# Linear attention of two mixing stages without chunk states, all convolution taps on VectorE, and a reordered last step

## The chip, the cores and the metric

One core of a Trainium2 chip runs the whole program. The metric is the device time of one execution in microseconds (us); lower is better. TensorE (PE) multiplies matrices, VectorE (DVE), ScalarE (ACT) and GpSimd (POOL) do elementwise work, SyncE (SP) issues the transfers of the weights. Semaphores order the engines among each other; each engine runs its own instructions strictly in program order.

## The reference

256 tokens of width 1024 go through two blocks of two layers each. The first block (a gated MLP, an attention with relative bias, two SwiGLU layers) is untouched. Each of the second block's two layers is a mixing stage and a gated feed-forward stage. A mixing stage projects the tokens with `w_in`, and then computes three things side by side: a causal depthwise convolution with 31 taps over 256 channels, then a layer norm; a causal softmax attention with 4 heads ("moba"); and a gated linear attention with 4 heads (key width 64, value width 128). Their outputs are joined and multiplied by `w_out`. The linear attention is, in the reference, in chunks of 32 tokens:

```
G = jnp.cumsum(gc, axis=3)                  # within a chunk
qg = qc * jnp.exp(G); kg = kc * jnp.exp(-G); kd = kc * jnp.exp(gamma - G)
attn = jnp.where(tril, einsum("bhnid,bhnjd->bhnij", qg, kg), 0.0)
d_state = einsum("bhnjd,bhnje->bhnde", kd, vc)
state <- decay[..., None] * state + d_state          # scan over 8 chunks
o = einsum("bhnij,bhnje->bhnie", attn, vc) + einsum("bhnid,bhnde->bhnie", qg, s_prev)
```

## The kernel before, in words

**Weights and tiles.** All weights come as a stream of 206 units of 128x2048 floats, each 1 MB, through four slots. For every unit U, ACT rounds it to fp32r (`hi(U)`, line 489), DVE forms the remainder (`lo(U)`, line 947), and PE uses both, with three products for each tile (`split3`, lines 1499 to 1501: hi times hi, hi times lo, lo times hi). SP issues the transfer of unit U+4 once `lo(U)` is done (line 341). PE can use a unit only after its `lo`, so the place of each `lo` in DVE's order is a due time for PE. Tokens lie in two halves of 128 (`m` = 0, 1).

**The mixing stage** (lines 1760 to 2020 on PE, one loop pass per layer `l`). U0 is its first unit. PE runs `step(0)` to `step(5)`, each a product of the tokens with 512 columns (step 4: 256), over 8 tiles `kt` for m0 and again for m1. Step 2 uses units U0+4 and U0+5, step 3 U0+6 and U0+7, step 4 U0+8, step 5 U0+9 and U0+10; each unit but U0+8 holds half of the `kt` (0 to 3 or 4 to 7). The dictionaries `m0`, `m1` of a step name small pieces of PE work that run behind a given `kt`. After step 5 comes `out_product` with units U0+11 to U0+14, turns (j, q), with hooks of its own.

**The small pieces on PE** are: `conv_turn` and `logits`; `cumsum` (line 1827, the running sum of the log gates by a product with the block-triangular `tri`); `qk_turn` (transposes of q and k); `kd_turn` (transposes of the decayed keys, kept by ACT as `kdt`); `gla_scores` (line 1844); `state_inc(n)` (line 1859, the increment of the state by chunk n, n = 0 to 6, each four products, each after the state two chunks back has been updated); `gla_out(b)` (lines 1885 and 1891: for each token half and head pair one product of the masked scores with the values, then one product for each of the chunks with its state, 28 in the two calls); `mqk_turn`, `moba_scores`, `moba_turn`, `moba_pv` for the softmax attention; `ln_turn`, `ln_back` around the layer norm of the convolution; `y_turn`, `mo_turn` for the outputs.

**DVE** runs, in one hand-written order (lines 1217 to 1420), the `lo` of units U0+2 to U0+16, the taps, the exponent products, the masking of the scores (`copy_predicated`, line 1286, eight of 128 columns), `state(n)` (lines 1299 and 1301), the softmax preparation `moba_begin`, and the head norms. A tap (lines 1242 and 1246) multiplies a shifted window of `hpad` by one weight and adds it to `cacc`: both inputs lie in SBUF. Of the 31 taps of the first 128 channels (a = 0) all are on DVE; of those of the second (a = 1), the first 20 are on **POOL** (`POOL_TAPS`, lines 444 to 452: a multiply into `ptap`, then an add into `cacc2`) and 11 on DVE, which then adds `cacc2` (line 1319). So DVE has 42 taps per layer, 22 of them alternating between the two halves, and 20 of the first half in a row.

**ACT** runs the `hi` of the units, copies PSUM results to SBUF (`keep`, line 766), and evaluates the exponentials and other functions.

Of the kernel before, what the change touches and what calls it, by code (L numbers as in the profile page):

```python
# [19 lines left out]
P = 128  # L20
# [8 lines left out]
SEQ = 256  # L29
# [14 lines left out]
NCH = SEQ // GCH  # L44
RANK = 16
# [17 lines left out]
POOL_TAPS = 20  # L63
# [14 lines left out]
def two_blocks_kernel(nc, x_in, stream, cols, bs_col, ws_t, gs_row, fin_row, fin2_row, rel_rows, ffn_cw,  # L78
                      conv_w, conv_ln, moba_g, gla_g, gate_w, gate_b, gate_in, out):
    ctx = ExitStack()  # L80
    with ctx:
# [33 lines left out]
        def const(name, shape, dt=F32):  # L115
# [7 lines left out]
        tri = const("tri", [P])  # L123
        ones = const("ones", [P])
# [11 lines left out]
        dec = const("dec", [2, NCH])  # L136
# [45 lines left out]
        kdt = at("kdt", [M, 256], o_sc + 5184)  # L182
# [3 lines left out]
        st_g = at("st_g", [NCH - 1, 2, P], o_sa)  # L186
# [14 lines left out]
        ptap = at("ptap", [SEQ], o_sc + 8768)  # L201
        cacc2 = at("cacc2", [SEQ], o_sb + 3200)
# [48 lines left out]
        x_qktr, x_G, x_e1, x_gd, x_e2, x_qg, x_kd, x_kdtr, x_kdc = (  # L251
            sem("gla_" + n) for n in ("qk_transposed", "G_kept", "exp_G", "G_diff", "exp_diff", "q_decayed", "k_decayed",
                                      "kd_transposed", "kd_kept"))
        x_at0, x_A, x_Am, x_dS, x_St, x_o, x_oc = (
            sem("gla_" + n) for n in ("masked_zeroed", "scores", "scores_masked", "state_inc", "state", "o", "o_kept"))
# [5 lines left out]
        x_pm, x_pa, x_tap1 = sem("conv_pool_product"), sem("conv_pool_sum"), sem("conv_tap_second")  # L261
# [90 lines left out]
        def _(pool):  # L352
# [13 lines left out]
            t3 = tri[:, :].rearrange("p (b c) -> p b c", c=GCH)  # L366
            pool.affine_select(out=t3, in_=t3, compare_op=ALU.is_ge, fill=0.0, base=0,
# [25 lines left out]
            pool.dma_start(glg[:, :, :], gla_g).then_inc(consts_loaded, 16)  # L393

# [33 lines left out]
            for l in range(2):  # L428
# [13 lines left out]

                pool.wait_ge(x_cpad, l + 1)
                for i in range(POOL_TAPS):
                    dst = ptap if i else cacc2
                    if i > 1:
                        pool.wait_ge(x_pa, (POOL_TAPS - 1) * l + i - 1)
                    pool.tensor_scalar(dst[:, :], hpad[:, 1, i:i + SEQ], cw[:, l, 1, i:i + 1], None,  # L448
                                       ALU.mult).then_inc(x_pm, 1)
                    pool.wait_ge(x_pm, POOL_TAPS * l + i + 1)  # L450
                    if i:
                        pool.tensor_tensor(cacc2[:, :], cacc2[:, :], ptap[:, :], ALU.add).then_inc(x_pa, 1)
# [22 lines left out]
        def _(act):  # L475
# [250 lines left out]
            for l in range(2):  # L726
# [25 lines left out]
                hi(U0 + 4)  # L752

# [7 lines left out]
                hi(U0 + 5)  # L761
# [13 lines left out]
                flat = [z[:, :, :].rearrange("p a t -> p (a t)") for z in (gG, eG, nG, dG)]  # L775
                act.activation(flat[0], tb[3][:, :], ACT.Copy).then_inc(x_G, 1)
                act.activation(flat[1], tb[3][:, :], ACT.Exp, scale=1.0 / TAU).then_inc(x_e1, 1)
                act.activation(flat[2], tb[3][:, :], ACT.Exp, scale=-1.0 / TAU).then_inc(x_e1, 1)
                hi(U0 + 7)
                act.wait_ge(x_gd, l + 1)  # L780
                act.activation(flat[3], flat[3], ACT.Exp, scale=1.0 / TAU).then_inc(x_e2, 1)
# [37 lines left out]
                moba_exp(0)  # L819
# [7 lines left out]

                o_keep(0)
                moba_exp(1)
                o_keep(1)  # L830
# [109 lines left out]
        def _(dve):  # L940
# [269 lines left out]
            for l in range(2):  # L1210
# [19 lines left out]
                first = [(0, i) for i in range(TAPS)]  # L1230
                second = [(1, i) for i in range(POOL_TAPS, TAPS)]
                order = []
                while first:
                    order += [first.pop(0)] + ([second.pop(0)] if second else [])

                def taps(n0, n1):
                    for a, i in order[n0:n1]:
                        src = hpad[:, a, i:i + SEQ]
                        w = cw[:, l, a, i:i + 1]
                        i0, done, n = (0, x_tap, TAPS) if a == 0 else (POOL_TAPS, x_tap1, TAPS - POOL_TAPS + 1)  # L1240
                        if i == i0:
                            dve.tensor_scalar(cacc[:, a, :], src, w, cw[:, l, a, TAPS:TAPS + 1], ALU.mult,
                                              ALU.add).then_inc(done, 1)
                        else:
                            dve.wait_ge(done, n * l + i - i0)
# [12 lines left out]
                lo(U0 + 5)  # L1258
                taps(9, 14)
# [8 lines left out]
                e4 = eG[:, :, :].rearrange("p a (n c) -> p a n c", c=GCH)  # L1268
                dve.tensor_copy(dec[:, :, :], e4[:, :, :, GCH - 1]).then_inc(x_qg, 1)
                dve.wait_ge(x_qktr, 2 * l + 2)  # L1270
                dve.wait_ge(x_qg, 3 * l + 1)
                ef, nf, df = (z[:, :, :].rearrange("p a t -> p (a t)") for z in (eG, nG, dG))
                dve.scalar_tensor_tensor(ef, tb[1][:, :], float(DK) ** -0.5, ef, ALU.mult, ALU.mult).then_inc(x_qg, 1)
                dve.tensor_tensor(nf, tb[2][:, :], nf, ALU.mult).then_inc(x_qg, 1)
                taps(14, 17)
# [867 lines left out]
```

## Time and profile before

| | |
|---|---|
| Time, median of 3 runs | 1272.89 us (1270.46 to 1273.14) |
| Time of the profiled execution | 1270.38 us, of which the span of the trace 1268.7 us |
| Busy PE / DVE / ACT / POOL | 1245.9 (98%) / 816.0 (64%) / 664.3 (52%) / 141.7 us (11%) |
| Granted clock of TensorE | full (2.4 GHz) throughout |
| Transfers | 220.13 MB, 174 GB/s on average |

The two mixing stages end their products at about 760 and 1066 us of the span; the stretches in question are 660 to 750 us (layer 0) and 967 to 1057 us (layer 1). In the rows, a start time is in us from the start of the span, then comes the duration; `x8` says that eight neighbouring records were merged. An fp32 product is two MATMUL records; a transpose and an fp32r product are one. The duration of a record holds its latency; what one costs in a row of many is the distance between starts.

### The profile page before, as it was taken

The page shows a single profiled execution, that of the slowest core. Times are in us where ns is not written, and L with a number is a line of the kernel's source. Part 1 is how long each engine was busy: PE and PEld are TensorE (multiplying, and loading weights), DVE is VectorE, ACT ScalarE, POOL GpSimd, SP SyncE. Part 2 cuts the span into 40 slices and gives each one's busy share as a digit, 9 for nine tenths or more (in the row PEclk, how much of TensorE's full clock was granted, in tenths as well). Part 3 has the DMA queues.
Part 4 walks back from the last instruction along what each step waited for, and adds up shares of the span by engine and source line. Part 5 has one row for each costly group of instructions (what it writes and reads, how often), then busy time and mean ns, then how long its engine had stood idle before and what let it go on. Part 6 is the DMA issues. An engine that isn't in the chain of part 4 may idle for free.

```text
span 1268.7 us, 16607 instructions
## 1 busy us (share of the span) xinstructions
PE 1245.9 (98%) x6276; PEld 1027.1 (81%) x6276; DVE 816.0 (64%) x926; ACT 664.3 (52%) x800; POOL 141.7 (11%) x164
## 2 busy tenths in 40 slices
PE   7999999999999989999999999999999999999998
PEld 5888888888898768888887788888888777888886
DVE  5466455545567565555469976777746987687763
ACT  6545264434366554444347356676536554666652
POOL 2000000000010000000029610000003930000000
PEclk9999999999999999999999999999999999999999
DMA  9544454446364236445634235544562424554440
GB/s 346 211 182 179 170 197 178 169 186 232 133 249 154 96 122 240 170 170 216 225 112 161 100 129 203 199 161 170 185 223 103 166 95 166 199 183 157 189 183 33
DMA packets 32534, 220.13 MB, mean 174 GB/s; under 512 B 4000, under 2 KB 4032, under 8 KB 6752
## 3 DMA queue, kind: packets, MB, share of 16 engines
q1 hardware_dynamic: 29952, 212.35, 45.2%
q0 software_dynamic: 1664, 5.41, 1.4%
q10 hardware_dynamic: 864, 1.61, 0.4%
q8 instruction: 39, 0.64, 0.2%
q14 instruction: 15, 0.12, 0.0%
HBM read 218.31 MB, written 1.05 MB: 173 GB/s over the span
## 4 chain that ended last, share of the span: by engine, by line
PE 95%; DVE 3%; ACT 1%; DMA 0%; issue 0%; POOLq 0%; POOL 0%; ACTq 0%
PE acc L1499 28%; PE acc L1501 27%; PE acc L1500 27%; PE tb L1531 5%; DVE wlo L947 1%; PE acc L1686 1%; PE acc L1688 1%; PE acc L1689 1%; DVE cacc L1246 1%; PE tb L1859 1%; PE tb L1600 1%; PE tb L1721 1%; PE acc L1885 0%; PE tb L1740 0%; PE acc L1891 0%; DMA x<-in_x_in 0%
## 5 line engine op out<-in xcount | busy, mean ns | idle before, releaser
L947 DVE TENSOR_TENSOR wlo<-raw,whi 128x2048 fp32r<-128x2048 f32 x200 | 458.1, 2310 | 237.4 <-ACT whi L489 237.4
L489 ACT ACTIVATE whi<-raw 128x2048 fp32r<-128x2048 f32 x200 | 376.8, 1907 | 109.2 <-PE acc L1501 100.9
L1499 PE MATMUL acc<-whi,xth 128*128 128x512 f32 (+1 forms) x1056 | 419.1, 397 | 4.4 <-DVE xtl L969 2.2
L1501 PE MATMUL acc<-whi,xtl 128*128 128x512 f32 (+1 forms) x1056 | 409.2, 387 | 0.0
L1500 PE MATMUL acc<-wlo,xth 128*128 128x512 f32 (+1 forms) x1056 | 408.4, 387 | 0.0
L1499 PEld LDWEIGHTS acc<-whi,xth 128*128 128x128 f32 x1056 | 198.7, 188 | 50.0 <-issue 5.8
L1501 PEld LDWEIGHTS acc<-whi,xtl 128*128 128x128 f32 x1056 | 198.6, 188 | 41.3
L1500 PEld LDWEIGHTS acc<-wlo,xth 128*128 128x128 f32 x1056 | 199.0, 188 | 36.8
L1499 PE MATMUL acc<-whi,yth 128*128 128x512 f32 x512 | 202.2, 395 | 1.7 <-DVE ytl L1380 1.7
L1501 PE MATMUL acc<-whi,ytl 128*128 128x512 f32 x512 | 199.7, 390 | 0.0
L1500 PE MATMUL acc<-wlo,yth 128*128 128x512 f32 x512 | 199.5, 390 | 0.0
L1499 PEld LDWEIGHTS acc<-whi,yth 128*128 128x128 f32 x512 | 96.2, 188 | 22.8 <-issue 3.7
L1501 PEld LDWEIGHTS acc<-whi,ytl 128*128 128x128 f32 x512 | 96.1, 188 | 20.4
L1500 PEld LDWEIGHTS acc<-wlo,yth 128*128 128x128 f32 x512 | 96.2, 188 | 19.0
L1428 DVE SCALAR_TENSOR_TENSOR cv<-tb,fcw,cv 128x255 f32<-128x255 f32 (+1 forms) x176 | 72.7, 475 | 14.5 <-ACT cv L875 11.9
L1070 DVE SCALAR_TENSOR_TENSOR yy<-acc,stat,sg 128x256 f32<-128x256 f32 x44 | 20.9, 479 | 80.6 <-ACT sg L596 80.6
L596 ACT ACTIVATE sg<-acc,stat 128x256 f32<-128x256 f32 x44 | 20.5, 472 | 88.8 <-PE acc L1501 88.7
L448 POOL TENSOR_SCALAR ptap<-hpad,cw 128x256 f32<-128x256 f32 x38 | 62.2, 1636 | 3.7
L494 ACT ACTIVATE xth<-xg 128x512 fp32r<-128x512 f32 x32 | 20.0, 633 | 78.2 <-DVE xg L957 78.2
L866 ACT ACTIVATE us<-acc,stat 128x512 f32<-128x512 f32 x44 | 30.5, 693 | 57.5 <-PE acc L1501 57.5
L373 POOL TENSOR_SCALAR stat<-stat 128x2 f32<-128x2 f32 x9 | 2.7, 295 | 418.3 <-ACT junk L503 418.3
L1246 DVE SCALAR_TENSOR_TENSOR cacc<-hpad,cw,cacc 128x256 f32<-128x256 f32 x80 | 48.7, 639 | 1.0
(238 smaller groups left out, 1030.2 us busy)
## 6 DMA issues: line engine op xcount, KB each, us to landing
raw<-in_stream SPq DMA_DIRECT2D x200, 1024.0 KB, 4.8
rb<-in_rel_rows POOLq DMA_DIRECT2D x8, 256.0 KB, 2.9
raw<-in_stream SPq DMA_DIRECT2D x4, 256.0 KB, 4.9
raw<-in_stream SPq DMA_DIRECT2D x2, 512.0 KB, 8.1
gs_sb<-in_gs_row POOLq DMA_DIRECT2D x1, 1024.0 KB, 5.4
frow<-in_fin_row POOLq DMA_DIRECT2D x2, 512.0 KB, 5.4
x<-in_x_in ACTq DMA_DIRECT2D x2, 256.0 KB, 5.0
x<-in_x_in ACTq DMA_DIRECT2D x1, 512.0 KB, 7.3
```

Source lines behind the costliest of these rows:

```text
L448: pool.tensor_scalar(dst[:, :], hpad[:, 1, i:i + SEQ], cw[:, l, 1, i:i + 1], None, ALU.mult).then_inc(x_pm, 1)
L489: act.activation(whi[:, s, :], raw[:, s, :], ACT.Copy).then_inc(hi_ready, 1)
L596: act.activation(sg[:, j % 2, m, :], pair_bank(j + pair, m)[:, 0:256], ACT.Silu, scale=rms(STATS[k], m)).then_inc(g_silu, 1)
L866: act.activation(us[:, j % 2, m, :], pair_bank(j + pair, m)[:, :], ACT.Copy, scale=rms(r1, m)).then_inc(f_ev, 1)
L947: dve.tensor_tensor(wlo[:, s, :], raw[:, s, :], whi[:, s, :], ALU.subtract).then_inc(lo_ready, 1)
L1070: dve.scalar_tensor_tensor(yy[:, j % 2, m, :], pair_bank(j + pair, m)[:, 256:512], rms(STATS[k], m), sg[:, j % 2, m, :], ALU.mult, ALU.mul ...
L1246: dve.scalar_tensor_tensor(cacc[:, a, :], src, w, cacc[:, a, :], ALU.mult, ALU.add).then_inc(done, 1)
L1428: o = dve.scalar_tensor_tensor(dst, src, fcw[:, l, bass.ds(16 * j + 4 * a + tap + 32 * t, 1)], dst, ALU.mult, ALU.add)
L1499: pe.matmul(o, xh, wh, start=first, stop=False)
L1500: pe.matmul(o, xh, wl, start=False, stop=False)
L1501: return pe.matmul(o, xl, wh, start=False, stop=last)
L1531: return pe.transpose(o, i, ident[0:n, 0:n])
```

## The change

It does three things.

1. **Linear attention without states.** `kd_turn`, `kdt`, `state_inc`, `state` and the products with the states are gone. The scores within a token half are completed instead: besides the old products of `nG` with `eG` (same chunk), there are products of the keys decayed to the end of their chunk (`dG`) with the queries of the next chunk (distance one, 16 small ones of 32x32), of `kB` with `qB` (the first two chunks with the last two, 8 of 64x64), and, for the first token half with the second, of `kC` with `qC` (4 of 128x128, kept by ACT as `aX`). `kB`, `qB`, `kC`, `qC` are `dG` and `eG` times a table of factors `ftab`, the exponential of 12 extra columns that `cumsum` gets from the widened constant `trb`; four DVE products make them. `gla_out` is then four products of the scores for each b, plus two of `aX`. The scores are masked by the whole triangle, with one `copy_predicated` for each b. `cumsum` now writes banks 0 and 1, the transposed q and k and the scores banks 2 and 3.
2. **All 62 taps on DVE**, alternating between the two channel halves; POOL has none. `cacc2`, `ptap` and the add of line 1319 are gone.
3. **Order.** `hi(U0+5)` on ACT comes before the logarithm of the gates, `lo(U0+4)` and `lo(U0+5)` on DVE before the first tap, all scores behind `kt` 3 of m1 of step 3. In step 5, both `gla_out` run earlier, `ln_turn` and the second `moba_scores` at the end of m0, the transposes and products of the softmax attention are moved to other `kt`, and `y_turn(0)` goes into the output product. ACT squares the head outputs (`o_square`), and does both `moba_exp` after them.

```diff
-POOL_TAPS = 20
@@ gpsimd
-                for i in range(POOL_TAPS):
...
-                    pool.tensor_scalar(dst[:, :], hpad[:, 1, i:i + SEQ], cw[:, l, 1, i:i + 1], None,
-                                       ALU.mult).then_inc(x_pm, 1)
...
-                        pool.tensor_tensor(cacc2[:, :], cacc2[:, :], ptap[:, :], ALU.add).then_inc(x_pa, 1)
@@ scalar
                 hi(U0 + 4)
+                hi(U0 + 5)
                 act.wait_ge(x_z, l + 1)
...
+                act.activation(ftab[:, :, :].rearrange("p (a m) c -> p (a m) c", m=M), Gt, ACT.Exp,
+                               scale=1.0 / TAU).then_inc(x_tab, 1)
...
                 hi(U0 + 8)
-                act.wait_ge(x_kdtr, l + 1)
-                act.activation(kdt[:, :, :].rearrange("p m c -> p (m c)"), tb[0][:, :], ACT.Copy).then_inc(x_kdc, 1)
                 hi(U0 + 9)
+                act.wait_ge(x_X, l + 1)
+                act.activation(aX[:, :, :, :].rearrange("p b a t -> p b (a t)"), tb01[:, :, 0:2 * P], ACT.Copy).then_inc(x_Xc, 1)
...
                 o_keep(0)
+                o_square(0)
+                o_keep(1)
+                o_square(1)
+                moba_exp(0)
                 moba_exp(1)
@@ vector
+                order = [(a, i) for i in range(TAPS) for a in range(2)]
...
+                lo(U0 + 4)
+                lo(U0 + 5)
                 dve.wait_ge(x_cpad, l + 1)
-                taps(0, 5)
-                lo(U0 + 4)
-                taps(5, 9)
+                taps(0, 9)
...
-                lo(U0 + 5)
-                taps(9, 14)
+                taps(9, 20)
                 lo(U0 + 6)
...
-                taps(14, 17)
+                taps(20, 26)
                 lo(U0 + 7)
...
+                dve.tensor_tensor(kb4, k5[:, :, 0:2, :], factor(0, 0, 2, 1), ALU.mult).then_inc(x_kb, 1)
+                dve.tensor_tensor(qb4, q5[:, :, 2:4, :], factor(2, 0, 2, 1), ALU.mult).then_inc(x_kb, 1)
+                dve.tensor_tensor(kc4, k5[:, 0:4:2, :, :], factor(4, 0, 4, 2), ALU.mult).then_inc(x_kb, 1)
+                dve.tensor_tensor(qc4, q5[:, 1:4:2, :, :], factor(8, 1, 4, 2), ALU.mult).then_inc(x_kb, 1)
+                taps(26, 36)
                 lo(U0 + 8)
...
+                taps(36, 42)
                 lo(U0 + 9)
-                state(0)
...
+                taps(42, 48)
                 lo(U0 + 10)
+                taps(48, 62)
@@ tensor
+                def gla_scores():
+                    pe.wait_ge(x_kb, 4 * l + 4)
...
+                    for m, a, b in both:
+                        c, t = (2 * m + a) * P, m * P
+                        for e in (0, 2 * GCH):
+                            k0, q0 = t + e, t + e + GCH
+                            pe.matmul(tb[2 + b][e:e + GCH, c + e + GCH:c + e + 2 * GCH], dG[rows[b], a, k0:k0 + GCH],
+                                      eG[rows[b], a, q0:q0 + GCH], start=True, stop=True)
...
-                step(3, m0={5: kd_turn}, end=all_of((gla_scores, (0,)), (gla_scores, (1,))),
-                     m1={5: lambda: state_inc(0)})
-                state_inc(1)
+                step(3, m1={3: gla_scores})
...
+                step(5, m0={1: lambda: gla_out(0), 3: lambda: moba_scores(0), 5: lambda: gla_out(1),
+                            7: all_of((ln_turn, ()), (moba_scores, (1,)))},
+                     m1={2: lambda: moba_turn(0), 4: ln_back, 5: all_of((moba_pv, (0,)), (moba_turn, (1,))),
+                         7: lambda: moba_pv(1)})
...
-                            pe.wait_ge(x_oc, 2 * l + 2)
+                            pe.wait_ge(x_osq, 2 * l + 2)
...
-                    (0, 2): lambda: y_turn(1), (1, 2): mo_turn})
+                    (0, 0): lambda: y_turn(0), (0, 2): lambda: y_turn(1), (1, 2): mo_turn})
```

## Rows read from the trace of the kernel before

**Rows 1.** The page: its first line, and the ended-last chain by engine.
```profile
span 1268.7 us, 16607 instructions
...
PE 95%; DVE 3%; ACT 1%; DMA 0%; issue 0%; POOLq 0%; POOL 0%; ACTq 0%
```

**Rows 2.** The waits of PE, whole span: total us, times, longest.
```profile
PE acc L1499 <- DVE wlo L947: 1.9, 2, 1.6
PE acc L1499 <- DVE ytl L1380: 1.7, 2, 0.9
```

**Rows 3.** Timeline of PE (start, duration, line) around the waits for `lo(U0+5)`.
```profile
678.10 0.39 PE L1501 MATMUL acc<-whi,xtl 128*128 128x512 f32 x1
680.13 0.50 PE L1499 MATMUL acc<-whi,xth 128*128 128x512 f32 x1 [1.65 <-DVE wlo L947]
...
987.00 0.50 PE L1499 MATMUL acc<-whi,xth 128*128 128x512 f32 x1 [0.29 <-DVE wlo L947]
```

**Rows 4.** The chain that ended last, 640 to 760 us: start, us, what.
```profile
694.51 0.44 PE tb L1531 x4
696.35 1.64 PE tb L1844 x16
...
702.30 0.58 PE tb L1859 x8
...
722.67 0.42 PE acc L1885 x2
723.09 0.35 PE acc L1891 x8
...
724.22 0.86 PE tb L1931 x8
```

**Rows 5.** Timeline of PE: around `state_inc(0)`, around `gla_out(0)`, first use of U0+7.
```profile
692.99 0.39 PE L1499 MATMUL acc<-whi,xth 128*128 128x512 f32 x1
...
701.91 0.39 PE L1501 MATMUL acc<-whi,xtl 128*128 128x512 f32 x1
...
702.81 0.50 PE L1499 MATMUL acc<-whi,xth 128*128 128x512 f32 x1
...
703.61 0.40 PE L1499 MATMUL acc<-whi,xth 128*128 128x512 f32 x1
...
721.11 0.45 PE L1885 MATMUL acc<-gv,aT 128*128 128x128 f32 x2
...
724.14 0.93 PE L1931 MATMUL tb<-mkT,mqT 64*128 64x128 f32 x8
```

**Rows 6.** Busy time of the instructions on `cacc`, in layer 0's stretch of taps.
```profile
669.55:720.90 51.35, 0.25 (x3) 0.28 (x4) 25.32 (x43) 15.87 (x19) 1.00 0.40 144
```

**Rows 7.** Timeline of DVE: `lo(U0+7)`; two taps and the add, POOL then idle.
```profile
689.27 2.82 DVE L947 TENSOR_TENSOR wlo<-raw,whi 128x2048 fp32r<-128x2048 f32 x1
...
719.16 0.48 DVE L1246 SCALAR_TENSOR_TENSOR cacc<-hpad,cw,cacc 128x256 f32<-128x256 f32 x1
719.68 0.48 DVE L1246 SCALAR_TENSOR_TENSOR cacc<-hpad,cw,cacc 128x256 f32<-128x256 f32 x1
720.09 0.42 DVE L1319 TENSOR_TENSOR cacc<-cacc,cacc 128x256 f32<-128x256 f32 x1
```

**Rows 8.** Timeline of DVE: eight taps of the feed-forward convolution, an input in PSUM.
```profile
785.25 3.34 DVE L1428 SCALAR_TENSOR_TENSOR cv<-tb,fcw,cv 128x255 f32<-128x255 f32 x8 [1.26 <-ACT cv L875]
```

**Rows 9.** Line 947, ns min/median/max: 400 to 640 us, then 676 to 700 us.
```profile
L947 DVE TENSOR_TENSOR wlo<-raw,whi x40: 2280/2291/2294, 398.3 to 638.5; 128x2048 fp32r<-128x2048 f32 x40
...
L947 DVE TENSOR_TENSOR wlo<-raw,whi x4: 2816/2824/2827, 677.3 to 696.9; 128x2048 fp32r<-128x2048 f32 x4
```

**Rows 10.** Timeline of POOL: multiplies of two taps.
```profile
678.03 2.84 POOL L448 TENSOR_SCALAR ptap<-hpad,cw 128x256 f32<-128x256 f32 x1
...
681.79 0.97 POOL L448 TENSOR_SCALAR ptap<-hpad,cw 128x256 f32<-128x256 f32 x1
```

**Rows 11.** Timeline of ACT behind the first softmax copies: table load; second softmax copies.
```profile
731.06 1.28 ACT L835 ACT_TABLE_LOAD   x1
...
735.33 0.60 ACT L813 ACTIVATE pt<-tb 128x512 f32<-128x512 f32 x1 [0.72 <-PE tb L1531]
```

More of the change, by code:

```diff
@@ L250, in two_blocks_kernel @@
                                       "log", "log_a", "cumsum"))
[L251 to L255, printed above, removed]
+        x_qktr, x_G, x_tab, x_e1, x_gd, x_e2, x_qg, x_kd, x_kb = (
+            sem("gla_" + n) for n in ("qk_transposed", "G_kept", "factors", "exp_G", "G_diff", "exp_diff", "q_decayed",
+                                      "k_decayed", "far_scaled"))
+        x_at0, x_A, x_Am, x_X, x_Xc, x_o, x_oc = (
+            sem("gla_" + n) for n in ("masked_zeroed", "scores", "scores_masked", "cross", "cross_kept", "o", "o_kept"))
         x_osq, x_oss, x_oms, x_or, x_ytr, x_yg, x_yh, x_yl = (
@@ L1228, in _ @@
                 o.then_inc(x_z, 1)
[L1230 to L1234, printed above, removed]
+                order = [(a, i) for i in range(TAPS) for a in range(2)]
                 def taps(n0, n1):
@@ L1239, in taps @@
                         w = cw[:, l, a, i:i + 1]
[L1240 to L1241 removed]
+                        done = x_tap1 if a else x_tap
+                        if i == 0:
                             dve.tensor_scalar(cacc[:, a, :], src, w, cw[:, l, a, TAPS:TAPS + 1], ALU.mult,
@@ L1848, in state_inc @@
-                def state_inc(n):
-                    m, p = n // 4, slice(GCH * (n % 4), GCH * (n % 4) + GCH)
-                    if n == 0:
-                        pe.wait_ge(x_kdc, l + 1)
-                        pe.wait_ge(x_ev, 10 * l + 4)
-                    if n >= 2:
-                        pe.wait_ge(x_St, (NCH - 1) * l + n - 1)
+                def gla_scores():
+                    pe.wait_ge(x_kb, 4 * l + 4)
+                    both = [(m, a, b) for m in range(M) for a in range(2) for b in range(2)]
+                    rows = [slice(DK * b, DK * b + DK) for b in range(2)]
+                    for m, a, b in both:
+                        c, ts = (2 * m + a) * P, slice(m * P, (m + 1) * P)
+                        pe.matmul(tb[2 + b][:, c:c + P], nG[rows[b], a, ts], eG[rows[b], a, ts], start=True, stop=True)
+                    for m, a, b in both:
+                        c, t = (2 * m + a) * P, m * P
[3 more added lines that the diff above has]
+                                      eG[rows[b], a, q0:q0 + GCH], start=True, stop=True)
+                    for m, a, b in both:
+                        c = (2 * m + a) * P
+                        mm = pe.matmul(tb[2 + b][0:2 * GCH, c + 2 * GCH:c + P], kB[rows[b], 2 * a + m, :],
+                                       qB[rows[b], 2 * a + m, :], start=True, stop=True)
+                        if m and a:
+                            mm.then_inc(x_A, 1)
@@ L1986, in _ @@
                                     wlo[:, s, ws], kt == 0, kt == KT - 1)
-                        if m == 0 and kt == 3:
-                            state_inc(2)
                     mm.then_inc(m0_done if m == 0 else unit_used, 1)
@@ L1991, in _ @@
                         mqk_turn()
-                        state_inc(3)
-                state_inc(4)
-                step(5, m0={1: lambda: state_inc(5), 3: all_of((state_inc, (6,)), (moba_scores, (0,))),
-                            5: all_of((ln_turn, ()), (gla_out, (0,)), (moba_scores, (1,))),
-                            7: all_of((gla_out, (1,)), (moba_turn, (0,)))},
-                     m1={1: ln_back, 3: all_of((moba_pv, (0,)), (moba_turn, (1,))), 6: lambda: moba_pv(1), 7: lambda: y_turn(0)})
+                step(5, m0={1: lambda: gla_out(0), 3: lambda: moba_scores(0), 5: lambda: gla_out(1),
+                            7: all_of((ln_turn, ()), (moba_scores, (1,)))},
+                     m1={2: lambda: moba_turn(0), 4: ln_back, 5: all_of((moba_pv, (0,)), (moba_turn, (1,))),
+                         7: lambda: moba_pv(1)})
                 def mix_ready(j):
```

159 lines of the change are left out of this document (64 added, 95 removed).

## The prediction

> **What bounds the kernel now.** I read the page first: the chain that ended last is 95% PE and 3% DVE [rows 1], so what counts is PE's work and the few places where PE waits. The waits of PE are next. In the whole span only two kinds touch the mixing stages: two for the remainder of a weight unit, together 1.9 us, and two for the last remainder of the linear attention's output, together 1.7 us [rows 2]. The first kind is `lo(U0+5)`: PE is through with unit U0+4 at 678.10 + 0.23 = 678.33 and goes on at 680.13, that is 1.80 lost with the restart; in layer 1 the row shows 0.29, with the restart 0.45 [rows 3]. In layer 1 PE comes 1.35 us later to the same place, because DVE's order there starts at the same event and PE has done more before it. Then I read DVE between 669.55 and 720.90: it has no gap there that matters, and the instructions on `cacc` alone, 43 of them, take 25.3 of its 51.35 us, 0.59 each [rows 6]. So DVE is the second limit: it is not waited for often, but it delivers the units only just in time. `lo(U0+7)` ends at 689.27 + 2.82 = 692.09 and PE wants it at 692.99 [rows 5, 7]. Whoever puts more on DVE there must say what comes off.
>
> **PE work, per layer.** Prices are distances on the path. An insertion among the large products also costs a lead and a slow restart: around `state_inc(0)` PE goes from 701.91 + 0.23 to 702.81, and the next three products take 0.80 instead of 0.68, so 0.67 + 0.12 = 0.79 for an insertion of which 0.58 is the work [rows 4, 5]. The overhead is then 0.2.
> Removed: `state_inc` seven times. Five stand alone at about 0.79, two share an insertion and cost about 0.68: 5.3 us. `gla_out` takes 721.11 to 724.14, 3.03, and the second call the same: 6.0 [rows 5]. `kd_turn` 0.44 [rows 4]. The old scores 1.64 + 0.2 = 1.85 [rows 4]. Sum 13.6.
> Added, scores: the old eight, 1.64 (0.205 each with 128 stationary columns [rows 4]); the four of `kC` at the same price, 0.82; the eight of 64x64 at the price of a state increment, 0.58 / 4 = 0.145: 1.16; the sixteen of 32x32. No row has that shape. The nearest is a product with a state, 32 stationary columns and 128 moving: four take 0.35, 0.09 each [rows 4]. Its upper bound is a full product, 0.205, its lower bound one half of the nearest row, 0.045. I take 0.10: 1.6. A change of shape also costs something: a full product between the small ones takes 0.42 instead of 0.205 [rows 4]; three such changes, 0.6, and the insertion 0.2. Sum 6.0, with bounds of 4.5 (small ones at 0.045, no cost for changes) and 8.2 (all at 0.205 with changes).
> Added, output: twelve full products at 0.205 = 2.46, and one more insertion than before, 0.2: 2.7.
> Net: 8.7 − 13.6 = −4.9 us per layer, between −6.4 and −2.7. The 12 extra columns of `cumsum` I cost at nothing: 16 records of 128 columns take 1.64, 0.10 each, well above what so few columns need while the stationary load sets the pace; if not, it is under 0.1.
> The Trainium skill (TensorE: Matmul & The Clock Gate, LDWEIGHTS) says that loading the stationary operand costs by its columns and not by its rows. The rows' falling prices for 128, 64 and 32 columns agree; an estimate from its formula would put the small products near 0.06 each and the sum lower by about 0.7 a layer.
>
> **The taps, and what POOL did to DVE.** Twenty more taps at 0.59 would be 12 us more on DVE, and that would sink the change. But the trace says that 0.59 is not the price of a tap. With POOL idle (from 718.9 on) a tap lasts 0.48; two in a row on the same sum start 0.52 apart (the second waits for the first), and the next instruction starts 0.41 behind [rows 7]. Eight taps of the feed-forward convolution, which alternate over four outputs, take 3.34, so 0.40 each [rows 8]. The new order alternates between two sums, so every tap finds its predecessor done. I take 0.40, with 0.52 as the upper bound; 62 taps are then 24.7 us, against 25.3 for 42 taps and the add. The cause is a lock between DVE and POOL: where they meet, a POOL multiply of 0.97 takes 2.84 while a `lo` runs [rows 10], and four `lo` in a row take 2.82 instead of 2.29 [rows 9]; those 4 x 0.53 = 2.1 us come back too.
> The Trainium skill (SBUF — State Buffer, Who interferes with whom) says that a DVE instruction with two SBUF inputs and a GpSimd instruction that reads SBUF exclude one another for their whole length. By that rule, the trace agrees, for taps and `lo` alike.
> DVE also loses the states (about 3.9 with the copy of the decay), 0.34 for the add and 1.2 for the square, which ACT takes; it gains four products of 256 columns, 1.4 at the 0.34 that the add occupies. So DVE has about 7 us less to do in each layer, though 20 taps more.
>
> **Due times, walked through in layer 0** (start 669.55, as before). On DVE: `lo(U0+4)` to 671.8 and `lo(U0+5)` to 674.0; 9 taps to 677.4, log gates 678.0, 11 taps 682.3, `lo(U0+6)` 684.6, three products 686.3, 6 taps 688.7, `lo(U0+7)` 691.0; the last decay product and the four new ones to 693.1, 10 taps 697.0, `lo(U0+8)` 699.2. On PE: unit U0+5 is there at 678.33, so the wait of 1.80 (0.45 in layer 1) is gone. `cumsum` at 679.7 finds its input of 678.1, 1.6 before. Step 3 starts at 688.4 (`lo(U0+6)` 684.6). **It wants `lo(U0+7)` at 691.1 and gets it at 691.0: no margin in layer 0, 1.4 in layer 1.** The scores at 696.5 find their four inputs of 693.1. The scores last to 702.5. Their mask waits for them on DVE from 699.2 to about 702: behind that wait are 26 taps and `lo(U0+9)`, `lo(U0+10)`; mask to 703.2, then 705.6, 707.8 (U0+9), 710.2, 712.4 (U0+10), last tap 718.0. PE wants U0+9 at 712.3 and U0+10 at about 717, and `ln_turn` comes at 721.4. All in time. ACT waits for the cross scores before it copies `aX`; behind it are both keeps of `mqk` and `hi(U0+10)`. That is 702.6 to 703.2 and not in the way: the second `mqk` is finished by PE only at 705.3.
> **What is late next.** The tail of step 5 is packed more tightly. After `ln_turn` come the statistics, the second softmax preparation, its exponentials and copy, then on ACT a table load, the silu and three more, 4.3 us, before the second softmax copy (731.06 to 735.33 [rows 11]). That chain is 10.1 us long after `ln_turn`, and PE has 9.6 of work: a wait of 0.5 before `moba_pv(1)`. From there to `y_turn(1)` DVE and ACT need 6.6 (hi, lo, gain, sums, gating), PE 6.15: another 0.5. Both are estimates by the same walk. The old wait of 0.9 for the last remainder [rows 2] stays: its loop behind `y_turn(1)` is unchanged.
> POOL's new memsets run once, among the loads of the constants, before anyone needs them: nothing.
>
> **Sum.** −2 x 4.9 = −9.8; −1.80 − 0.45 = −2.25; new waits 2 x 1.0 = +2.0. Together −10.0. The profiled execution took 1270.4, so 1260.4; against the median of the runs, 1272.9, it would be 1262.9. The profiled time lies at the lower edge of the runs, so I put the forecast between: **1261.5**, own range 1257.5 to 1265.5.
>
> **Rivals.**
> *DVE becomes the bound* (slower). If the slow taps were not POOL's doing, 62 taps at 0.60 would put `lo(U0+7)` at 696.1, 5.0 us after PE wants it, and the last tap at 727.8, 6.4 after `ln_turn` is due; `moba_begin(0)` is queued behind the taps, one more us. The output product would go on at about 748.9 where it does at 746.9 now: +2 per layer, 1274.5 on the profiled scale, 1275.5 forecast. It decides from about 0.57 per tap. For it: 0.59 is what 42 taps show [rows 6]. Against: 0.48 and 0.40 where POOL is idle or the second input is not SBUF [rows 7, 8]. Chance 0.07.
> *Half way*: taps at 0.52, as for two on one sum. 24 such taps before `lo(U0+7)` are 2.9 late, 1.5 in layer 1, and as the last tap then ends just as `ln_turn` is due, about 5 us of the gain go: 1266.5. A variant of it is the Trainium skill's rule (VectorE: DVE Perf Modes, The DRAIN you can't avoid) that the next instruction does not start before the pipe is empty. In this kernel that would be 0.48 per tap, the duration in [rows 7], 1.9 us more before `lo(U0+7)`, and 1264.5; the 0.40 of [rows 8] speaks against it. Chance 0.07 for the first, 0.04 for the variant.
> *The small products are dear*: scores at 8.2 instead of 6.0, +2.2 per layer, 1266. Chance 0.08.
> *Several unseen waits in the repacked step 5*, 4 us and more per layer, so that nothing measurable is left: 1270 to 1272. For it: every due time there is my walk, and ACT's order in that stretch is new. Chance 0.04.
> *The forecast*: 0.70.
>
> **How the numbers follow.** From the low bound of the small products (−1.5 a layer, 1258) with a little more, 1257, to the half-way and dear cases with some of their spread, 1268: outside are the slow rival and no change, and a little below. A difference under 0.2% (2.5 us) can't be told from none. Slower by more than that 0.07; within it 0.04; the rest, faster, 0.89.
>
> **What would show it.** Taps of about 0.40 and `lo` of 2.29 throughout the stretch; no wait for `lo(U0+5)`; a wait of at most some tenths for `lo(U0+7)`; the scores in one block of about 6.0 us and `gla_out` of about 1.3 each; waits of about 0.5 at `moba_pv(1)` and `y_turn(1)`. Layer 0 shorter by about 5.7, layer 1 by about 4.3. It is wrong if taps stay near 0.6, if PE waits for `lo(U0+7)` by microseconds, or if the scores take 8.

## The result and the profile after

| | before | after |
|---|---|---|
| Median | 1271.73 us (1270.46 to 1273.14, 4 runs) | 1256.78 us (1254.33 to 1257.39, 4 runs) |
| Ratio, 95% interval | | 0.9877 (0.9865 to 0.9889) |
| Profiled execution, span | 1268.7 us | 1252.6 us |

The change takes 15.0 us off where 11.4 were forecast. The time, 1256.78, lies 0.2 us below the widest range of the prediction (1257 to 1268) and 0.7 below the one that stands with its sum (1257.5 to 1265.5). Of the 11.4, the worked sum gave 10.0; the rest came from putting the forecast between the profiled execution and the median. The page after, its first two lines and the chain by engine:

```profile
span 1252.6 us, 16325 instructions
...
PE 1230.3 (98%) x6172; PEld 1020.8 (81%) x6172; DVE 803.5 (64%) x928; ACT 665.6 (53%) x806; POOL 45.7 (4%) x92
...
PE 94%; DVE 3%; ACT 2%; issue 0%; DMA 0%; POOLq 0%; POOL 0%; DVEq 0%; ACTq 0%
```

PE still sets the time (compare [rows 1]). It has 15.6 us less to do, and DVE, with 40 taps more in the two layers, has 12.5 less (about 14 were forecast). Where the time goes is seen in the stretch that the change touches. I take it from the first product of the gate to the start of `mo_turn`, in both layers: first before, then after. Each line gives the start and end, the length, the busy time of PE with its records, and the granted clock (1.00 is the full 2.4 GHz).

```profile
660.13:751.07 90.94, 88.42 (x555) 1.00 0.36 128
968.35:1057.94 89.59, 88.44 (x555) 1.00 0.36 130
```

```profile
660.38:742.51 82.13, 80.71 (x503) 1.00 0.40 141
959.84:1041.88 82.04, 80.62 (x504) 1.00 0.39 142
```

The stretches are 8.81 and 7.55 shorter, together 16.4, against 16.1 in the span: nothing else of note changed. These two lengths are the finer measure below, because the executions of one kernel differ by 2 to 3 us. The traces show a reason outside the stretches: in seven of the experiments TensorE's granted clock falls to 1.2 GHz for 3.4 us or more at 447 to 449 us, behind a wait of 2.9 us, and in the other runs, with the same wait, it doesn't. Two experiments have such a fall inside a stretch as well; it is named there.

The waits of PE after, those in the stretch:

```profile
PE acc L1491 <- DVE ytl L1372: 1.8, 2, 0.9
...
PE tb L1523 <- DVE og L1359: 1.1, 2, 0.5
```

Each line gives the total in us, the times and the longest. The wait for a unit [rows 2] is gone, the old one of 0.9 per layer for the last remainder stands, and 0.5 per layer before `y_turn(1)` is new. The scores on PE (layer 0), from the start of the block to the next large product:

```profile
696.96 1.16 PE L1831 MATMUL tb<-eG,nG 64*128 64x128 f32 x16
698.06 0.46 PE L1836 MATMUL tb<-eG,dG 64*32 64x32 f32 x32
698.44 0.68 PE L1840 MATMUL tb<-qB,kB 64*64 64x64 f32 x16
699.05 0.71 PE L1846 MATMUL tb<-qC,kC 64*128 64x128 f32 x8
699.70 0.50 PE L1491 MATMUL acc<-whi,xth 128*128 128x512 f32 x1
```

By the distances between starts: 1.10 for the eight full products (1.64 before [rows 4]), 0.38 for the sixteen small ones, 0.61 for the eight of 64x64, 0.65 for the last four; 2.74 in all. With 0.09 between the last large product and the block, and 0.12 for the large products' slow restart behind it, it is 2.95. The forecast had 6.0. Here is the error.

On DVE, all taps and the `lo` between them:

```profile
L1258 DVE SCALAR_TENSOR_TENSOR cacc<-hpad,cw,cacc x120: 464/477/502, 674.9 to 1014.1; 128x256 f32<-128x256 f32 x120
...
L963 DVE TENSOR_TENSOR wlo<-raw,whi x3: 2281/2282/2284, 682.6 to 697.3; 128x2048 fp32r<-128x2048 f32 x3
...
709.88 5.65 DVE L1258 SCALAR_TENSOR_TENSOR cacc<-hpad,cw,cacc 128x256 f32<-128x256 f32 x14
715.43 0.43 DVE L1321 SCALAR_TENSOR_TENSOR pp<-tb,cmask 128x256 f32<-128x256 f32 x1
```

Fourteen taps in 715.43 − 709.88 = 5.55, 0.396 each; `lo` at 2.28; before, with POOL at work, they took 0.59 and 2.82 [rows 6, 9].

### The profile page after: what moved, and what is told of

It reads as the page before. It is cut to its first block, busy times and chain, and to the rows that moved or that the text cites. A ratio compares the mean times of both kernels' runs of the same rounds, so it can differ in the third digit from the quotient of the medians.

```text
span 1252.6 us, 16325 instructions
## 1 busy us (share of the span) xinstructions
PE 1230.3 (98%) x6172; PEld 1020.8 (81%) x6172; DVE 803.5 (64%) x928; ACT 665.6 (53%) x806; POOL 45.7 (4%) x92
## 4 chain that ended last, share of the span: by engine, by line
PE 94%; DVE 3%; ACT 2%; issue 0%; DMA 0%; POOLq 0%; POOL 0%; DVEq 0%; ACTq 0%
PE acc L1491 27%; PE acc L1493 27%; PE acc L1492 27%; PE tb L1523 5%; PE acc L1678 1%; PE acc L1680 1%; PE acc L1681 1%; DVE wlo L963 1%; ACT whi L493 1%; PE tb L1592 1%; PE tb L1713 1%; PE tb L1732 0%; DMA x<-in_x_in 0%; ACT pp L814 0%; PE acc L1871 0%
## 5 line engine op out<-in xcount | busy, mean ns | idle before, releaser
L891 ACT ACTIVATE cv<-tb,fcw 128x256 f32<-128x256 f32 x88 | 42.6, 565 | 10.5 <-PE tb L1523 10.5
L969 DVE TENSOR_TENSOR x<-acc,x 128x512 f32<-128x512 f32 x32 | 21.7, 685 | 25.5 <-PE acc L1493 25.5
```

Source lines behind the costliest of these rows:

```text
L891: o = act.activation(cv[:, j % 2, a, :], tb[2 * (j % 2) + a // 2][:, (a % 2) * SEQ:(a % 2 + 1) * SEQ], ACT.Identity, scale=fcw[:, l, bass. ...
L969: dve.tensor_tensor(xs, out_bank(OUT_PAIR[k], m, c)[:, :], xs, ALU.add).then_inc(n_add, 1)
```

## The experiments

The theory after the result: the walk on DVE was right, and the scores were over-priced, because (A) products that alternate between two row groups (the halves of 64 rows, `b` = 0 and 1) overlap the load of one with the work of the other, and (B) small products are cheap. Rival causes: sizes alone; less lost to DVE than thought; the new order worth more than I gave it. Unless said otherwise, an experiment changes the kernel after, and the lengths of its two stretches stand against 82.13 and 82.04: "+0.94 and +0.93" means layer 0 and layer 1, in us. Medians stand against 1256.78.

**The order of the row groups.**

```diff
-                    both = [(m, a, b) for m in range(M) for a in range(2) for b in range(2)]
+                    both = [(m, a, b) for b in range(2) for m in range(M) for a in range(2)]
```

> The changed kernel with one edit: the scores are computed for all of the first row group (partitions 0 to 63) and then for all of the second (64 to 127), in each of their first three parts, instead of alternating. Same products, same shapes. Theory A (the alternation of row groups lets the load of one product's stationary operand overlap the other's work): the eight full products go from 1.10 back to 1.64 us as in the kernel before, the 64x64 ones from 0.61 to about 1.1, the small ones from 0.38 to about 0.6 or more; the block of scores from 2.74 to about 4.0, +1.3 us per layer, +2.5 in all (1259.3). Theory B (the scores are cheap because of their sizes, not their order): the block stays at 2.7 and the time at 1256.8.

```profile
699.81 1.71 PE L1831 MATMUL tb<-eG,nG 64*128 64x128 f32 x16
701.45 0.60 PE L1836 MATMUL tb<-eG,dG 64*32 64x32 f32 x32
701.98 0.96 PE L1840 MATMUL tb<-qB,kB 64*64 64x64 f32 x16
702.87 0.72 PE L1846 MATMUL tb<-qC,kC 64*128 64x128 f32 x8
703.52 0.50 PE L1491 MATMUL acc<-whi,xth 128*128 128x512 f32 x1
```

The eight full products are back at 1.64, to the hundredth, the small ones take 0.53, the middle ones 0.89; the block is 3.71, +0.97. The stretches are +0.94 and +0.93. The median, 1257.28 us, does not resolve it. Order counts, with 0.97 of the 3.05 us that were missing per layer; the rest are prices of small and middle products that are below the forecast's in either order, and the 0.6 for changes of shape.

How the order acts can be read from the starts of the single records. The two lines show the records that are under way at one moment of the eight full products, first in the kernel after, then here:

```profile
697.18 0.39 PE L1831 MATMUL tb<-eG,nG 64*128 64x128 f32 x4
700.14 0.38 PE L1831 MATMUL tb<-eG,nG 64*128 64x128 f32 x2
```

In the kernel after, the starts come in pairs, 0.007 apart, with 0.112 from pair to pair. Here they come singly, 0.112 apart, and a second series, also at 0.112, starts at 700.36 while the first still has three records to start. So a row group keeps the same pace in both orders; what the alternation does is to let both groups work side by side from the first product on, and here they do so only where the series happen to meet. Theory A is right that the groups overlap, but it is more than a load behind a product: the products themselves run together. The old price of 0.205 was thus an average of stretches with one group and with two.

**The same in the kernel before**: its eight score products alternate.

```diff
-                step(3, m0={5: kd_turn}, end=all_of((gla_scores, (0,)), (gla_scores, (1,))),
+                step(3, m0={5: kd_turn}, end=gla_scores,
```

(with `gla_scores` looping over `m`, `a`, `b`, the latter innermost; one execution)

> The kernel before with one edit: its eight score products alternate between the two row groups. Theory A: they take 1.1 instead of 1.64 us, -0.5 per layer. Theory B: they stay at 1.64, as the shapes are unchanged. One us in all is too little for the whole time; the block in the profile decides.

```profile
698.98 1.16 PE L1844 MATMUL tb<-eG,nG 64*128 64x128 f32 x16
700.08 0.50 PE L1499 MATMUL acc<-whi,xth 128*128 128x512 f32 x1
```

1.10 where it was 1.64 [rows 4]: 0.137 per product instead of 0.205, for shapes and data that are the same. The starts show the same two patterns, pairs every 0.112 here and single records 0.112 apart before.

The Trainium skill says (TensorE: Matmul & The Clock Gate, The mechanism) that a stationary load overlaps running products only if it goes to another row group. Both runs agree that a change of row group makes such products faster, and the prediction had passed that sentence over. The "only" isn't borne out: the large products of 256 columns use all rows, start 0.12 apart after the block of scores, and have a load record of 0.19 each between them.

The 0.54 did not reach the time. The stretches are 90.98 and 89.67, so +0.04 and +0.08 against the kernel before, where the expectation had 0.5 less per layer. PE comes earlier to the state increments and waits for DVE there, 0.3 us in each layer, which is new:

```profile
PE tb L1860 <- DVE st_g L1299: 0.7, 2, 0.3
```

**The price of the small products**: the sixteen issued five times over (one execution).

```diff
-                    for m, a, b in both:
+                    for m, a, b in 5 * both:
```

> The changed kernel, with the sixteen 32x32 products issued five times over (the same result is written again). It measures their price: 64 more per layer. By the changed kernel's profile (0.38 us for 16, 0.024 each) the set of 80 takes 1.9 us, +1.5 per layer, +3.1 in all. By the price that the prediction took from the nearest row (0.10 each) it would be 8 us for 80, +6.4 per layer, +13 in all; by its lower bound (0.045) 3.6.

```profile
700.09 1.56 PE L1836 MATMUL tb<-eG,dG 64*32 64x32 f32 x160
701.57 0.68 PE L1840 MATMUL tb<-qB,kB 64*64 64x64 f32 x16
```

Eighty take 1.48, so 64 more cost 1.10, 0.017 each, and layer 0's stretch is +1.10. The prediction had 0.10 each and a lower bound of 0.045. The single records agree: four start within 0.02, and the next four 0.032 later, and a product is two records, so one costs 0.016. In layer 1 the stretch is +3.50: a gap that no semaphore explains lies among the small products there.

```profile
1000.45 1.52 PE L1836 MATMUL tb<-eG,dG 64*32 64x32 f32 x156
1004.23 0.25 PE L1836 MATMUL tb<-eG,dG 64*32 64x32 f32 x4 [2.26 <-issue]
...
q8 instruction: 1, 0.02, 4.1%
```

It is in no other kernel's list of PE's waits, and the granted clock is full there. The last line is from the transfers between 1001 and 1003 us: one of 16 KB on the queue for instructions, started at 1001.58, lasting 1.30 us. In layer 0 such a transfer started at 701.72, behind the small products. That would fit a long run of short products that gets ahead of the supply of its instructions, but no run varies it, so the cause stays open.

**Changes of shape**: full and small products mixed (one execution).

```diff
+                            for b in range(2):
+                                pe.matmul(tb[2 + b][:, c:c + P], nG[rows[b], a, ts], eG[rows[b], a, ts], start=True,
...
+                            for e in (0, 2 * GCH):
+                                k0, q0 = t + e, t + e + GCH
+                                for b in range(2):
```

> The changed kernel with the full and the 32x32 score products mixed (two full, four small, four times over), row groups still alternating. The prediction charged 0.2 us for each change of shape, seen around the full products of the old output, which use all 128 rows. If shape changes cost that, seven more changes add about 1.4 us per layer to the block of scores (2.74 to 4.1, +2.8 in all). If it was not the shape but the rows (a product over all 128 rows shares rows with its neighbours, so its load can't overlap them), nothing changes: 2.7, the full and small ones together about 1.5.

```profile
699.99 0.49 PE L1833 MATMUL tb<-eG,nG 64*128 64x128 f32 x4
700.41 0.26 PE L1838 MATMUL tb<-eG,dG 64*32 64x32 f32 x8
...
702.46 0.68 PE L1843 MATMUL tb<-qB,kB 64*64 64x64 f32 x16
```

Full and small together take 2.47 instead of 1.48, and the stretches are +0.95 each. With six more changes of shape (seven in place of one) that is 0.16 for each: between my two theories, nearer to the first. So shapes do matter, if less than the 0.2 charged, and the change keeps their number to three.

**GpSimd's taps back**: the second part undone, 20 taps on POOL and 42 on DVE.

```diff
-                taps(0, 9)
+                taps(0, 6)
...
+                dve.tensor_tensor(cacc[:, 1, :], cacc[:, 1, :], cacc2[:, :], ALU.add).then_inc(x_tap1, 1)
```

(and POOL's loop of the kernel before)

> The changed kernel with its second part undone: 20 taps of the second channel half on GpSimd again, 42 on VectorE in the old order and the add behind them, spread over the same places in proportion. If the lock between the two engines was what made a tap 0.6 us: taps at 0.60 and the remainders of units that GpSimd meets at 2.8; lo(U0+7) ends about 693 and PE waits for it by 1 to 2 us in layer 0; GpSimd ends its taps at about 719, when ln_turn is due at 718.5, another 1 us: +2 to +5 us (1259 to 1262). If the taps' price does not depend on GpSimd: VectorE has 20 taps less at 0.40, is early everywhere, and only GpSimd's end counts: +0 to +2.

```profile
680.26 4.80 DVE L1276 SCALAR_TENSOR_TENSOR cacc<-hpad,cw,cacc 128x256 f32<-128x256 f32 x8
684.98 2.83 DVE L977 TENSOR_TENSOR wlo<-raw,whi 128x2048 fp32r<-128x2048 f32 x1
...
694.38 0.50 PE L1513 MATMUL acc<-whi,xth 128*128 128x512 f32 x1 [1.28 <-DVE wlo L977]
```

1261.33 us, 4.6 above the kernel after; stretches +3.10 and +1.85. Eight taps take 4.72, 0.59 each, alternating as they do in the kernel after, where they take 0.40. Alternating alone does not make them fast; POOL has to be silent as well. With 20 taps fewer DVE is later, and PE waits for it. The wait shown is for `lo(U0+7)`. There is none for `lo(U0+5)`, although the taps are slow: the third part of the change, which puts that `lo` ahead of the taps, removes it by itself.

**The second part alone**, in the kernel before.

```diff
-POOL_TAPS = 20
...
+                order = [(a, i) for i in range(TAPS) for a in range(2)]
...
-                taps(17, 24)
+                taps(22, 34)
```

> The kernel before with the second part of the change alone: all 62 taps on VectorE, alternating, none on GpSimd; the states, scores and order as before, taps spread over the old places. Theory A (a tap costs 0.40 without GpSimd): VectorE is no later anywhere than before although it has 20 taps more, lo(U0+5) ends about 678.2, so the wait for it shrinks from 1.8 us to about 0 in layer 0 and from 0.45 to 0 in layer 1, and PE's work is unchanged: -2 us (1269 to 1270.5). Theory B (a tap costs 0.6 wherever it is): +12 us of work on VectorE per layer, PE waits by several us: 1280 and more.

1270.27 us beside 1272.52, ratio 0.9983 (0.9973 to 0.9992). The stretches are 1.76 and 0.75 shorter than before, and neither wait of PE for a unit is listed. So moving 20 taps onto the busier of two engines made the kernel faster by about what I had booked for the waits (1.80 and 0.45).

**Taps in a row**: first one channel half, then the other.

```diff
-                order = [(a, i) for i in range(TAPS) for a in range(2)]
+                order = [(a, i) for a in range(2) for i in range(TAPS)]
```

> The changed kernel with the taps in another order: 31 of one channel half, then 31 of the other, so each waits for the one before it. The prediction priced that at 0.52 per tap against 0.40. If so, lo(U0+7) comes about 3 us later, PE waits for it 2.7 us in layer 0 and 1 to 2 in layer 1, and the last tap ends 7 us later, about 722.5, 4 us after ln_turn is due, of which 3 are taken up by the earlier wait: +3 to +4 per layer, +6 to +8 in all (1263 to 1265). If the distance stays 0.40, no change.

```profile
674.63 4.13 DVE L1258 SCALAR_TENSOR_TENSOR cacc<-hpad,cw,cacc 128x256 f32<-128x256 f32 x8
678.68 0.68 DVE L1268 SCALAR_TENSOR_TENSOR la<-la,tmp 128x512 f32<-128x512 f32 x1
...
PE acc L1491 <- DVE wlo L963: 4.2, 2, 2.8
...
695.00:698.40 3.40, 3.40 (x9) 0.50 0.90 308
```

1265.64 us, +8.9; stretches +5.51 and +3.79. A tap costs 4.05 / 8 = 0.51, as read from [rows 7], and PE waits 2.8 and 1.4 us for `lo(U0+7)`, then for the last tap and for ACT's softmax copies. The price was right, its consequence somewhat worse than expected (9.3 in the two stretches for 6 to 8); the prediction's half-way rival gave this case 5. The last line shows a side effect: behind the wait of 2.8 the granted clock fell to 0.50 (1.2 GHz) for 3.4 us, and eight large products took 3.39 where eight take 1.82 at full clock. Little of it counts: the last tap ended at 722.66 and `ln_turn` began at 723.01, so at full clock PE would have waited for the tap instead. Behind the wait of 1.4 in layer 1 the clock did not fall.

**The order of the first units undone.**

```diff
-                lo(U0 + 4)
-                lo(U0 + 5)
                 dve.wait_ge(x_cpad, l + 1)
-                taps(0, 9)
+                taps(0, 5)
+                lo(U0 + 4)
+                taps(5, 9)
```

> The changed kernel with the order of the first units undone: lo(U0+4) behind 5 taps, lo(U0+5) behind the log gates, hi(U0+5) behind the logarithm. With fast taps lo(U0+5) ends at about 678.2, when PE wants it at 678.6 (layer 0 of the changed kernel), so almost nothing: within 0.5 us (1256.3 to 1257.3). If the new place of lo(U0+5) was what removed the wait of 1.8 + 0.45 us, +2 us (1259).

1256.64 us; stretches +0.40 and −0.03, and no wait for `lo(U0+5)` is listed. Its earlier place is worth nothing that the median shows and at most 0.4 us in layer 0: the fast taps remove that wait too. With slow taps (above) the place alone does. Either suffices, and the two gains don't add.

**Step 5's order undone.**

```diff
-                step(5, m0={1: lambda: gla_out(0), 3: lambda: moba_scores(0), 5: lambda: gla_out(1),
-                            7: all_of((ln_turn, ()), (moba_scores, (1,)))},
+                step(5, m0={3: lambda: moba_scores(0), 5: all_of((ln_turn, ()), (gla_out, (0,)), (moba_scores, (1,))),
+                            7: all_of((gla_out, (1,)), (moba_turn, (0,)))},
```

> The changed kernel with step 5's order undone: the small pieces of PE, and the copies and exponentials on ACT, at the places of the kernel before; y_turn(0) before the output product. If the new order is worth something, it is by the waits behind ln_turn, which comes two tiles earlier in the old order but finds everything else later: I expect within 1 us of the changed kernel, either way (1255.8 to 1257.8). Rival: the old order makes ACT's second output copy wait as before, 1 us per layer more (1259).

```profile
PE tb L1523 <- DVE cacc L1258: 2.0, 2, 1.2
```

1255.99 us; stretches +0.37 and 0.00. `ln_turn` now waits for the last tap (2.0 in all), and the wait before `y_turn(1)` is gone in exchange. Of the third part, these two places are worth at most 0.4 us each, and only in layer 0. The place of all the scores behind `kt` 3 of m1 was not undone, so nothing is shown about it.

**Two tries at the waits that are left.** In both, the square of the softmax outputs comes ahead of `hi(U0+12)`. First, `lo(U0+12)` later:

```diff
                 gated(0)
-                lo(U0 + 12)
-                y_gain(0)
...
+                y_gain(0)
                 gated(1)
+                lo(U0 + 12)
                 y_lo(0)
```

> A try at the waits left behind moba_pv(1). On ACT the square of the softmax outputs comes before hi(U0+12) instead of behind it, on VectorE lo(U0+12) comes behind the second gating instead of before the first gain. If the chain hi, lo, gain, sums, gating is what y_turn(1) waits for, its wait of 0.5 us per layer goes, and the one for the last remainder (0.9 per layer) shrinks or stays, as lo(U0+12) is now in its chain: -1 us in all, 1255.8. Rival: lo(U0+12) behind the gating makes the last remainder 1 to 2 us later, and the loss there eats the gain: 1256.8 to 1258.

```profile
PE acc L1491 <- DVE ytl L1372: 5.1, 2, 2.6
```

1261.98 us, ratio to the kernel before 0.9915 (0.9901 to 0.9929). The wait for `y_turn(1)` went, the one behind it grew from 0.9 to 2.6. The unit had only been moved from one chain into the next. The stretches are +2.43 and +1.01. In layer 0 the granted clock fell to 0.50 for 3.4 us behind the wait, and seven large products took 3.04 where they took 1.69 in layer 1 behind the same wait; without these 1.35, it is +1.08 and +1.01. So the rival had the right direction, and 2.1 us where it said up to 1.2; the rest of the 5.2 us in the median isn't explained by the stretches.

Then, earlier than both chains, in gaps where ACT and DVE stand idle:

```diff
                 o_square(0)
+                hi(U0 + 12)
                 o_keep(1)
...
                 dve.tensor_scalar(stat[:, 80:88], stat[:, 96:104], 1.0 / DV, EPS, ALU.mult, ALU.add).then_inc(x_oms, 1)
+                lo(U0 + 12)
...
                 gated(1)
+                y_gain(0)
                 y_gain(1)
+                y_lo(0)
...
-                    (0, 0): lambda: y_turn(0), (0, 2): lambda: y_turn(1), (1, 2): mo_turn})
+                    (0, 0): lambda: y_turn(0), (0, 1): lambda: y_turn(1), (1, 2): mo_turn})
```

> The changed kernel with unit U0+12 handled early instead of late: its hi on ACT right behind the first o_square, where ACT stands idle for 4 us, its lo on VectorE behind the sums of the head norm; both gains behind the second gating, and y_turn(1) one quarter earlier in the output product. The walk from the changed kernel's rows: the softmax square ends 730.7, its sums 731.5, gating 732.6, y_turn(1) at 733.3 without a wait, the last remainder 735.7, before PE wants it at 736.5. So both waits (0.54 and 0.88 per layer) go: -2.8 us in all, about 1254.0. Rival: the lo delays the first gating or the POOL root, and y_turn(0) waits instead: no gain.

> The changed kernel as it is, on the same chip and beside the same runs of the kernel before: the reference for the run above. 1256.8 us, as measured first, within the spread of a chip (1255.5 to 1258).

1251.44 us, ratio to the kernel before 0.9836 (0.9822 to 0.9849), beside 1255.56 for the kernel after, measured next to it on the same chip. The stretches are 80.73 and 80.62, −1.40 and −1.42, together the −2.8 expected. PE's list has neither wait any more; this is DVE there, where the unit now fits in:

```profile
726.45 0.17 DVE L1349 TENSOR_SCALAR stat<-stat 128x8 f32<-128x8 f32 x1
726.53 2.28 DVE L963 TENSOR_TENSOR wlo<-raw,whi 128x2048 fp32r<-128x2048 f32 x1
```

It is the fastest kernel of this study. The edit moves the unit, both gains and `y_turn(1)` together; which of them is needed was not tried apart.

## Why the prediction was wrong, point by point

**Wrong: the added scores.** This is the step that failed. The sum had 5.8 for the block and 0.2 for the insertion; measured are 2.74 and 0.21, 3.05 less per layer, 6.1 in all. By terms: the eight full products 1.10 instead of 1.64, the sixteen small 0.38 instead of 1.6, the eight of 64x64 0.61 instead of 1.16, the four of `kC` 0.65 instead of 0.82, and no separate 0.6 for the changes, which these distances already hold. Two things were wrong in it. "The old eight, 1.64" took a price from instructions of the same shape in another order; the alternation of the row groups was in the diff, and it is worth 0.54 there and 0.97 in the whole block. And the small shapes were priced by rows of other shapes: "its lower bound one half of the nearest row, 0.045" was a guess where nothing bounded from below. The range was cut at that bound. The small ones, the largest term of the error, cost 0.024 each, and 0.017 at the margin. The prediction's own estimate of 0.06 is what one series of them costs (two records 0.032 apart); four series side by side make it a quarter. With the measured block in place of 6.0 the sum is 10.0 + 6.1 = 16.1, against 16.4 in the stretches.

**Right in sum, wrong in its parts: the new waits**, booked at 0.5 before `moba_pv(1)` and 0.5 before `y_turn(1)`.

```profile
734.47 0.39 PE L1493 MATMUL acc<-whi,ytl 128*128 128x512 f32 x1
...
735.81 0.47 PE L1491 MATMUL acc<-whi,yth 128*128 128x512 f32 x1
```

From the last large product ahead of `moba_pv(1)` to the first behind it are 1.73 (728.30 to 730.03), where the kernel before, without a wait, has 1.49 (737.17 to 738.66); around `y_turn(1)` 1.34 (the lines above), where it has 0.59 (743.77 to 744.36). So the two cost 0.24 and 0.75, together the 1.0 forecast: that they make it up so exactly is luck. `cumsum`, taken as free, takes 0.95 instead of 0.89 in the chain of waits, 0.1 in the two layers and within the bound given. That leaves 16.0 against 16.4; the 0.4 between them is not traced.

**Right: PE's removed work** (13.6 per layer). No experiment took it off alone, but the two traces give it, each insertion counted from the last large product ahead of it to the pace of the large products behind it. In layer 0 of the kernel before, the seven `state_inc` take 5.3, `kd_turn` 0.45, the old scores 1.85 and the two `gla_out` 6.0, together 13.6; the two new `gla_out` take 2.7, as forecast.

**Right: DVE's taps and POOL's lock.** Taps at 0.40 (0.396), `lo` at 2.28, no wait for `lo(U0+5)`; the three runs on the taps (GpSimd's taps back, the second part alone, taps in a row) bear out 0.59 with POOL, 0.40 without, 0.51 in a row. The variant in which a tap costs its whole duration is out: the durations are 0.477, the starts 0.396 apart.

**Right: the walk.** After, DVE starts it 0.26 later than before (669.81 for 669.55). `lo(U0+7)` ended at 691.24 and PE took it up at 691.33, with at most 0.08 lost; the prediction had 691.0 and 691.1 with "no margin". The scores started at 696.96 (696.5), `y_turn(1)` waited 0.54 by the list of waits (0.5; 0.75 with what surrounds it, as above), the last remainder 0.88 (0.9). Behind the scores everything came about 3 us earlier than in the walk, as their block was 3 us shorter: the taps were done by 715.53 (718.0), `ln_turn` began at 718.45 (721.4).

**The rivals**: none of them came true, and none of those that I listed was on the fast side. All of them made the change worse, while the largest unknown, the price of products that no row showed, could also fall short.

**The reordering** was taken into the sum with the waits of 1.80 and 0.45, and they did go, but the fast taps alone remove them as well (the second part alone: 1.76 and 0.75), so the order added next to nothing.

## What to carry to other kernels

When an engine's instructions look slow, see what the neighbouring engine does at that time before pricing more of them: here the second engine's help cost the first more than it gave. Price a product by rows of the same shape *and* the same sequence of row groups; alternate two halves of 64 rows wherever the data allow it, and check that the next engine in line can use the time won (in the kernel before it couldn't). A large instruction that sat in a late chain here gained when it went into an idle gap ahead of that chain, and lost when it went to its end. And before a stretch is compared with another, look at the granted clock in both.

## What the runs showed of the hardware that I had not expected

Eight fp32 products over 64 rows with 128 stationary columns cost 0.205 us each on average if the row groups follow one after the other, and 0.137 if they alternate; in either case the records of one group start 0.112 apart. Products of 32x32 over 64 rows cost 0.024 alternating, 0.033 otherwise, and 0.017 for each further one in a run of 80. Turning between the two shapes six times more cost 0.99 us. In one layer of one kernel a run of 80 such products stopped for 2.26 us without a wait. And behind waits of 2.8 and 2.6 us TensorE's granted clock fell to 1.2 GHz for 3.4 us in layer 0 of two kernels, which lengthened the products there by 1.57 and 1.35, while behind the same wait of 2.6 in layer 1 it did not.
